# An RWKV-7 and pooling step on one core: 16x16 triangular inverses on VectorE, each pair's first steps begun in the pair ahead, other orders at the front and before the gate

## The chip, the core and the metric

The kernel runs on one core of a Trainium2 chip. Five engines work side by side, each through its own list of instructions: TensorE (PE in the profile; PEld is its weight load), VectorE (DVE), ScalarE (ACT), GpSimd (POOL) and SyncE (SP, which here issues DMAs). They meet at semaphores: an instruction raises one by 1 (a DMA by 16) when it ends, another waits until it has reached a number. The metric is device time of one execution in microseconds (us).

## The reference, cut to what matters

One layer for 256 prompt tokens and 8 short sequences of 8 sample tokens, 320 tokens in all, width 2048, in float32:

```
h = rmsnorm(x);  z = h @ w_in            # r, k, v, g, u, g_pool (1024 columns each), two gates (2048 each)
r, k, v = token shift of z's first 3072 columns
decay = exp(-0.606531*sigmoid(w0 + tanh(xw@w1)@w2));  a = sigmoid(a0 + (xa@a1)@a2)
kk = k*k_k / norm(k*k_k per head);  k = k*(1+(a-1)*k_a)
per head, per token: S = S*diag(decay) - (S kk)(kk*a)^T + v k^T;  o = S r
y_a = (groupnorm(o)*ln_w + ln_b + bonus*v) * silu(g)
y_b = windowed means of u, mapped, * silu(g_pool)
m = sigmoid(gate_a)*(y_a @ wa) + sigmoid(gate_b)*(y_b @ wb)
x = x + rmsnorm(m @ w_out);  x = x + sigmoid(x @ w_ple_gate) * (p @ w_ple)
```

The recurrence is worked in chunks of 64 tokens. Within a chunk the removal terms make a strictly triangular 64x64 matrix A per head, and the chunk needs (I - A)^-1, the matrix Y of the code.

## The kernel before, in words

**Splits.** The big products are taken in three passes: weights and activations are each split into a high and a low part, and hi·hi, hi·lo and lo·hi are added in PSUM. A weight chunk is 8 k-tiles by 128 columns. SP loads it (`wraw`), ACT casts its high part (`wh`, L682), DVE subtracts to get the low part (`wl`, L1017), and PE uses both (L1529 to L1531). There are four slots; ACT and DVE work three chunks ahead (`go(j)`, `ahead`). What PE does for one k-tile of a chunk, three matmuls, is called a unit below.

**Pairs.** The 16 heads are worked as 8 pairs of two heads. Pair r's recurrence runs while PE streams the 6 projection tiles (k, r, v, g, u, g_pool; 96 units) of the pair after it. `mix` exists once per engine. In PE's `mix` the small products stand in the code at fixed places, and `st.advance(AFTER[name])` puts so many units of the stream behind each. `tile_out` (`out(n)`) empties tile n from PSUM on DVE; the stream's next use of that bank waits for it (`acc_free`).

**One pair, in PE's order.** Two products for decay and a (L1632); the key norm (L1637), whose sum DVE takes on with a maximum, ACT with a root and DVE with a reciprocal (L1160); the turned values; the bonus sum (L1647); the products with the initial states (`z`, L1655), which wait for `zr`; the scores (L1661, L1666, L1671), for five groups of 64 tokens, four of the prompt and one of the samples; the turned keys; the inverse; then the chain over the four prompt chunks, outputs, mean (L1756), variance (L1759). The pair's end on DVE is `dO` (L1298), a reciprocal of the deviation (L1306), two steps of the norm, `yf`, and `out(5)` (L1044).

**The inverse.** DVE solves the 8x8 blocks on the diagonal by 23 dependent steps (shuffles within 32 partitions, multiplies, reductions; L1187 to L1245). Then three levels double the block: PE multiplies (`products`, L1688), DVE masks, PE multiplies again (`update`, L1695), DVE adds. The sample group needs none of the levels.

**Beside it.** POOL copies parameters and values, forms `kf`, `sg`, `aS*pi`, `zr`, `kBD`, issues the loads of the next pair and stores states. Before the pairs a front normalises x, transposes and splits h, and streams the first pair's tiles with the two low-rank maps (L1618) beside the later ones. After the pairs come pooling, the merge, the output projection, the last norm and the gate of the per-layer embedding.

Of the kernel before, what the change touches and what calls it, by code (L numbers as in the profile page):

```python
# [28 lines left out]
ds = bass.ds  # L29
# [27 lines left out]
LEVELS = 3  # L57
OCT = 8

# [18 lines left out]
BASE_STEPS = 23  # L78
# [23 lines left out]
def _columns(table, *widths):  # L102
    at = 0
    for name, width in widths:
# [6 lines left out]
                ("batch", NB), ("count", 4 * 16), ("upper", 1), ("lowers", 1), ("unit", 4), ("octs", OCT))  # L111
# [4 lines left out]
def shape_constants():  # L116
# [25 lines left out]
    put(CF, f, "octs", (row // OCT)[:, None] == np.arange(C // OCT)[None])  # L142
# [11 lines left out]
    put(CM, m, "inner", (s // OCT == t // OCT) & (s < t) & seq)  # L154
    a = CM["level"][0]
    for n in range(LEVELS):
        m[:, a + n * TP:a + (n + 1) * TP] = level(OCT * 2 ** n).reshape(P, TP)

# [9 lines left out]
def build(nc, x_prompt, x_sample, state_wkv, state_shift, state_pool, p_prompt, p_sample, norm_pre, norm_post,  # L168
# [3 lines left out]
    with ExitStack() as ctx:  # L172
# [43 lines left out]
        cur_m = r1.take("cur_m", [P, NPAR])  # L216
        lw2 = r1.take("lw2", [RANK, P])
# [66 lines left out]
        O_s, dO, dsq, sd, gsig = cl, pd, pi, kf, rn  # L284
        terms = r1.take("terms", [P, G, 5, 4])
        scratch = Region(used["rn"][0])
        inner = scratch.take("inner", [P, G, OCT])
# [6 lines left out]
        assert scratch.next <= used["rn"][1]  # L294
        parts = at(used["cl"][0], "parts", [P, G, 5, 4])
# [41 lines left out]
        wple0 = r4.take("wple0", [P, 7, 2 * P])  # L337
        wple1 = at(used["cm"][0], "wple1", [P, 5, 2 * P])
# [3 lines left out]
        def embedding_weights(m):  # L342
            if m < 2:
                return wple[:, m, :]
            if m < 9:
                return wple0[:, m - 2, :]
            return wple1[:, m - 9, :] if m < 14 else wple2[:, m - 14, :]
# [20 lines left out]
        for name in """y_out0 y_out1 root_table lo_ready x_in0 x_in1 x_in2 eout sout const_in rows_in rows2_in lora_in map_in filled  # L368
            last_done rows_out cur_p_ready lw2_in s0_in s0d_ready par_done xw_ready xw_used cur_m_ready acc_free vbd_ready
# [4 lines left out]
            vs_ready bt_ps y_ready ybd_ready x_ready base_step kt_ps tail_ps s_ready sd_ready endbd_ready  # L374
# [44 lines left out]
        def _(sp):  # L419
# [18 lines left out]
            row = 0  # L438
            for v in (norm_pre[0].rearrange("(q p) -> q p", p=P), norm_post[0].rearrange("(q p) -> q p", p=P),
                      mu_lora[0].rearrange("a (q p) -> (a q) p", p=P)[0:32, :], pool_scale[0].rearrange("(q p) -> q p", p=P)):  # L440
                n = v.shape[0]
                sp.dma_start(rows[row:row + n, 1, :], v).then_inc(s["rows2_in"], 16)
                row += n
# [55 lines left out]
        def _(pool):  # L499
# [8 lines left out]
            gp_.memset(stat[:, 3:4], 1.0).then_inc(s["filled"], 1)  # L508

            def pair_params(q):  # L510

                gp_.tensor_copy(cur_p[:, :], par[:, :].rearrange("p (n q) -> p n q", q=PAIRS)[:, :, ds(q, 1)]
                                .rearrange("p n q -> p (n q)")).then_inc(s["cur_p_ready"], 1)

# [16 lines left out]
            pair_params(0)  # L531
            pool.wait_ge(s["hT_ps"], 12)
# [22 lines left out]
            def mix(r):  # L555

                gp_.tensor_copy(cur_m[:, :], par[:, :].rearrange("p (n q) -> p n q", q=PAIRS)[:, :, ds(r, 1)]
                                .rearrange("p n q -> p (n q)")).then_inc(s["cur_m_ready"], 1)
                wait_alone("cur_m_ready", r + 1)

                wait_alone("acc_free", r * TILES_STEP + (ACC_STEP + TILES_STEP))
# [10 lines left out]

                wait_alone("sg_ready", r + 1)
                gp_.tensor_tensor(sg[:, :], sg[:, :], gS[:, :], ALU.mult).then_inc(s["sgs_ready"], 1)
# [40 lines left out]
            with pool.Fori(1, PAIRS) as q:  # L615
                r = q - 1
                wait_alone("acc_free", q * TILES_STEP + ACC_STEP)
                pair_params(q)
                mix(r)
# [3 lines left out]
                pair_loads(q)  # L623
                mix_out(r)
# [6 lines left out]
            pool.wait_ge(s["y_done"], PAIRS)  # L631
            pool.dma_start(spt[:, :], state_pool[0].rearrange("b t c -> (b t) c")).then_inc(s["pool_in"], 16)
# [40 lines left out]
        def _(act):  # L673
# [84 lines left out]

            def mix(r, q):
# [7 lines left out]
                go(0)  # L767
                act.wait_ge(s["cur_m_ready"], r + 1)
                A.activation(sq[:, :], kS[:, :], ACT.Square, scale=cur_m[:, K_K:K_K + 1]).then_inc(s["ksq_ready"], 1)
                act.wait_ge(s["lora2_ps"], r + 1)  # L770
                A.activation(pm[:, :], B[0][:, 0:T], ACT.Sigmoid, bias=cur_m[:, W0:W0 + 1]).then_inc(s["decay_in"], 1)
                A.activation(aS[:, :], B[1][:, 0:T], ACT.Sigmoid, bias=cur_m[:, A0:A0 + 1]).then_inc(s["a_ready"], 1)
                A.activation(sg[:, :], gS[:, :], ACT.Sigmoid).then_inc(s["sg_ready"], 1)
                act.wait_ge(s["kk_max"], r + 1)
                A.activation(rn[:, :], rn[:, :], ACT.Sqrt).then_inc(s["kk_norm"], 1)
                act.wait_ge(s["cum_ready"], r + 1)
                A.activation(pi[:, :], cl[:, :], ACT.Exp, scale=DECAY).then_inc(s["exp_ready"], 1)
# [29 lines left out]

                act.wait_ge(s["bt_ps"], r + 1)
                A.copy(BtBD[:, :, :, :].rearrange("p g h c -> p (g h c)"), B45[:, 0:2 * TP])

                act.wait_ge(s["kt_ps"], r + 1)
                A.copy(KtBD[:, :, :, :].rearrange("p g h c -> p (g h c)"), B23[:, 0:2 * TP])
                for n in range(LEVELS):
                    go(4 + n)
                out(2)
                go(4 + LEVELS)
# [193 lines left out]
        def _(dve):  # L1010
# [12 lines left out]
            def tile_out(q, n):  # L1023
# [13 lines left out]
                else:  # L1037
# [4 lines left out]
                    else:  # L1042
                        dve.wait_ge(s["gsig_ready"], q)
                        V.tensor_tensor(t[:, where], bank, gsig[:, :], ALU.mult).then_inc(s["acc_free"], 1)  # L1044
# [46 lines left out]
            for c in range(4):  # L1091
# [3 lines left out]
                if c == 0:  # L1095
                    split_lo(0, 0)
            split_lo(0, 1)
            split_lo(0, 2)

# [15 lines left out]
            split_lo(0, 3)  # L1115
# [23 lines left out]

            def mix(r, q):  # L1140
                def go(j):
                    ahead(q * CH_STEP + BASE_STEP, j)
# [4 lines left out]
                go(0)  # L1147
                dve.wait_ge(s["s0_in"], r * 128 + 128)
                for h in range(2):
                    V.transpose(S0T[half(h), :, half(h)], S0n[half(h), :, :]).then_inc(s["s0t_ready"], 1)  # L1150

                dve.wait_ge(s["kk_ps"], r + 1)
                V.tensor_scalar(rn[:, :], B[2][:, 0:T], 1e-24, None, ALU.max).then_inc(s["kk_max"], 1)

                dve.wait_ge(s["decay_in"], r + 1)
# [102 lines left out]
                for n in range(LEVELS):  # L1258
# [5 lines left out]
                    if n == 2:  # L1264
                        out(2)
# [695 lines left out]
```

## Time and profile before

| | |
|---|---|
| median of 3 runs (lowest to highest) | 1218.7 us (1217.64 to 1219.46) |
| profiled execution | 1217.77 us, of which the span of its instructions is 1216.2 us |
| PE busy | 1188.5 us, 98% of the span |
| DVE, ACT, POOL busy | 730.3 us (60%), 544.1 us (45%), 198.5 us (16%) |
| mean granted TensorE clock | 0.997 of full speed |
| share of the end chain on PE | 93% |

The span runs from the first to the last instruction. "Idle before" and the bracket behind a row say how long the engine had stood still before that instruction and what ended the stand. PE's matmuls are pipelined and their ends are modelled, so a PE that is shown busy can still hold short waits; those are found from the distance between the starts of two products and the units between them.

### The profile page before, as it was taken

Reading aid. Unit: us, or ns where it says so; the run is one execution under the profiler, and the core shown is the slowest. Engines: PE = TensorE matmul, PEld = TensorE weight load, DVE = VectorE, ACT = ScalarE, POOL = GpSimd, SP = SyncE. Lnnn points to the kernel's source line nnn. Section 1 sums busy time; section 2 is a strip of 40 time slices with the busy share of each in tenths; the row PEclk is TensorE's granted clock in tenths of the full one; section 3 lists DMA queues with packets and bytes.
Section 4 is the critical chain, followed back from the end, with each engine's and each line's share of the span. In section 5 each row is a group of like instructions: output and inputs, shape, how many; then the busy total and the mean of one; then the engine's idle time right before and its main releaser. Section 6 shows DMA issues by size and latency. Waiting matters only on the chain.

```text
span 1216.2 us, 21935 instructions
## 1 busy us (share of the span) xinstructions
PE 1188.5 (98%) x8060; PEld 1142.6 (94%) x8060; DVE 730.3 (60%) x1246; ACT 544.1 (45%) x875; POOL 198.5 (16%) x305
## 2 busy tenths in 40 slices
PE   4999999999999999999999999999999999999998
PEld 3789999999999999999999999999999999979998
DVE  6858584857668585867758744444444354475442
ACT  5244463737364563736353333333333343345342
POOL 3233141504123150503122000000000400000000
PEclk8999999999999999999999999999999999999999
DMA  9714333332433434332445465554545964424551
GB/s 231 191 53 117 97 98 105 90 103 80 131 96 98 113 84 117 91 104 79 122 116 171 122 173 145 148 152 141 155 138 156 253 189 138 138 71 132 160 160 49
DMA packets 279770, 155.37 MB, mean 128 GB/s; under 512 B 7717, under 2 KB 275661, under 8 KB 279076
## 3 DMA queue, kind: packets, MB, share of 16 engines
q1 hardware_dynamic: 272528, 139.65, 41.0%
q0 software_dynamic: 7056, 15.17, 5.0%
q8 instruction: 25, 0.41, 0.1%
q14 instruction: 13, 0.11, 0.0%
q10 hardware_dynamic: 148, 0.04, 0.0%
HBM read 149.45 MB, written 5.61 MB: 127 GB/s over the span
## 4 chain that ended last, share of the span: by engine, by line
PE 93%; DVE 3%; DMA 2%; ACT 1%; issue 0%; POOL 0%; SPq 0%; ACTq 0%; DVEq 0%; POOLq 0%
PE acc L1529 19%; PE acc L1530 19%; PE acc L1531 18%; PE wide L1531 5%; PE wide L1530 5%; PE wide L1529 5%; PE wide L1548 2%; PE wide L1695 2%; PE wide L1688 2%; PE wide L1618 1%; PE wide L1903 1%; PE wide L1655 1%; DMA pt<-in_p_sample 1%; PE wide L1661 1%; PE wide L1743 1%; PE wide L1666 1%
## 5 line engine op out<-in xcount | busy, mean ns | idle before, releaser
L1017 DVE TENSOR_TENSOR wl<-wraw,wh 128x1024 fp32r<-128x1024 f32 x256 | 313.7, 1230 | 219.7 <-ACT wh L682 212.1
L682 ACT CAST wh<-wraw 128x1024 fp32r<-128x1024 f32 x256 | 266.8, 1047 | 246.5 <-PE acc L1531 153.6
L1529 PE MATMUL acc<-hh,wh 128*128 128x320 f32 (+1 forms) x1084 | 362.1, 334 | 2.7 <-DVE wl L1017 2.7
L1530 PE MATMUL acc<-hl,wh 128*128 128x320 f32 (+1 forms) x1084 | 336.6, 311 | 0.0
L1531 PE MATMUL acc<-hh,wl 128*128 128x320 f32 (+1 forms) x1084 | 336.2, 310 | 0.0
L1529 PEld LDWEIGHTS acc<-hh,wh 128*128 128x128 f32 x1084 | 204.7, 189 | 6.7 <-issue 3.2
L1530 PEld LDWEIGHTS acc<-hl,wh 128*128 128x128 f32 x1084 | 204.5, 189 | 3.4
L1531 PEld LDWEIGHTS acc<-hh,wl 128*128 128x128 f32 x1084 | 203.9, 188 | 0.0
L1529 PE MATMUL acc<-x1h,wh 128*128 128x320 f32 x256 | 82.5, 322 | 0.4 <-DVE x1l L1486 0.4
L1529 PE MATMUL acc<-mh,wh 128*128 128x320 f32 x256 | 80.6, 315 | 0.0
L1531 PE MATMUL acc<-x1h,wl 128*128 128x320 f32 x256 | 79.1, 309 | 0.0
L1531 PE MATMUL acc<-mh,wl 128*128 128x320 f32 x256 | 79.1, 309 | 0.0
L1530 PE MATMUL acc<-ml,wh 128*128 128x320 f32 x256 | 79.1, 309 | 0.0
L1530 PE MATMUL acc<-x1l,wh 128*128 128x320 f32 x256 | 79.1, 309 | 0.0
L1531 PE MATMUL wide<-hh,wl 128*128 128x320 f32 x192 | 59.5, 310 | 0.0
L1530 PE MATMUL wide<-hl,wh 128*128 128x320 f32 x192 | 59.3, 309 | 0.0
L1529 PE MATMUL wide<-hh,wh 128*128 128x320 f32 x192 | 59.2, 308 | 0.0
L660 POOL DMA_DIRECT2D xt<-in_x_prompt x1 | 0.6, 557 | 301.6 <-PE wide L1531 301.6
L1529 PEld LDWEIGHTS acc<-x1h,wh 128*128 128x128 f32 x256 | 48.1, 188 | 1.4 <-DVE x1l L1486 0.7
L1529 PEld LDWEIGHTS acc<-mh,wh 128*128 128x128 f32 x256 | 48.0, 188 | 0.9
L1530 PEld LDWEIGHTS acc<-x1l,wh 128*128 128x128 f32 x256 | 48.1, 188 | 0.7
L1530 PEld LDWEIGHTS acc<-ml,wh 128*128 128x128 f32 x256 | 48.1, 188 | 0.0
(361 smaller groups left out, 2178.9 us busy)
## 6 DMA issues: line engine op xcount, KB each, us to landing
wraw<-in_w_in SPq DMA_DIRECT2D x160, 512.0 KB, 3.8
wraw<-in_w_branch SPq DMA_DIRECT2D x32, 512.0 KB, 4.0
wraw<-in_w_out SPq DMA_DIRECT2D x32, 512.0 KB, 4.0
wraw<-in_w_ple_gate SPq DMA_DIRECT2D x32, 512.0 KB, 4.1
xt<-in_x_prompt SPq DMA_DIRECT2D x2, 1024.0 KB, 6.9
S0n<-in_state_wkv POOLq DMA_DIRECT2D x64, 32.0 KB, 4.3
out<-so POOLq DMA_DIRECT2D x16, 128.0 KB, 2.8
xt<-in_x_prompt POOLq DMA_DIRECT2D x2, 1024.0 KB, 7.6
```

The lines of the kernel that those rows point to most:

```text
L682: A.copy(wh[:, slot, :], wraw[:, slot, :]).then_inc(s["hi_ready"], 1)
L1017: V.tensor_tensor(wl[:, slot, :], wraw[:, slot, :], wh[:, slot, :].bitcast(F32), ALU.subtract).then_inc(s["lo_ready"], 1)
L1529: M.matmul(out[:, 0:width], wh[:, slot, wcol], hi, start=first, stop=False)
L1530: M.matmul(out[:, 0:width], wh[:, slot, wcol], lo, start=False, stop=False)
L1531: return M.matmul(out[:, 0:width], wl[:, slot, wcol], hi, start=False, stop=last)
L1548: return M.transpose(out, in_, ident[0:rows, 0:rows])
L1618: M.matmul(B[n % 2][0:RANK, 0:T], (lw1, la1)[n % 2][:, k, :], xw[:, n % 4, :], start=k == 0, stop=k == KT - 1).then_inc(s["xw_used"], 1)
L1655: last = M.matmul(B45[:, P * b:P * b + 2 * TB + C], S0T[:, b, :], zr[:, b, :], start=True, stop=True)
L1661: last = M.matmul(B01[:, P * g:P * (g + 1)].rearrange("p (a c) -> p a c", a=2), flat(bBD, g), ar[:, :, tok(g)], start=True, stop=True)
L1666: last = M.matmul(B23[:, P * g:P * (g + 1)].rearrange("p (a c) -> p a c", a=2), flat(kBD, g), ar[:, :, tok(g)], start=True, stop=True)
L1688: last = M.matmul(B[0][:, tok(g)], flat(ABD, g), Y[:, g, :], start=True, stop=True)
L1695: last = M.matmul(B[1][:, tok(g)], flat(XBD, g), Tm[:, g, :], start=True, stop=True)
```

## The change

**Inverse.** `LEVELS` goes from 3 to 2. DVE solves 16x16 blocks: the 8x8 solution is followed by one more doubling on DVE, with 24 more steps (`BASE_STEPS` 23 to 47), among them 16 shuffles of 40 columns. `ABD` and the third score group are formed for the four prompt groups only. `ARK` and `AKBD` move out of that chain into the two levels; the weight splits go(4) and out(1) move into it.

**Pair.** The key squares, decay, a and gate sigmoids of the next pair (ACT: `key_squares`, `decays`, `gates`), and the turned states, norm maximum, running sum and its difference (DVE: `states_turned`, `decays`) stand inside the pair ahead. POOL takes the next pair's first parameters once `out(2)` of this one is done, copies the values after `out(4)`, and has a small third copy, `cur_n`, for the norm's weights. The units behind PE's places change with it. The key transposes move behind the first `products`.

**Front and ramp.** The four parameter rows go from SP's queue to POOL's. DVE splits weight chunks 1 and 3 earlier. Before the gate, two of the embedding products stand ahead of the sum for the last norm.

```
-LEVELS = 3
+LEVELS = 2
+HEX = 16
...
-            AFTER = dict(maps=13, key_norm=6, values=4, bonus=9, scores=8, keys=2, product=3,
-                         update=2, chain_rhs=2, chain_u=2, chain_state=1, mean=4, chain_end=3, inner=6)
+            AFTER = dict(maps=2, key_norm=8, values=10, bonus=9, scores=30, product=3,
+                         update=2, chain_rhs=2, chain_u=2, chain_state=1, mean=3, chain_end=3)
...
-                for g in range(G):
+                for g in range(GP):
                     last = M.matmul(B[4][:, tok(g)], flat(aBD, g), bU[:, tok(g)], start=True, stop=True)
...
+                stepped(25)
+                dve.sem_inc(s["waits"], 1)
+                for k in range(OCT):
+                    V.stream_shuffle(rows8[:, :, k, :], octo[:, :, :], hex_row(OCT + k)).then_inc(s["base_step"], 1)
+                V.tensor_scalar(sixteen[:, :, 0:OCT], octo[:, :, :], cfs("upper8"), None, ALU.mult).then_inc(s["base_step"], 1)
+                V.tensor_scalar(parts8[:, :, OCT, :], octo[:, :, :], cfs("lower8"), None, ALU.mult).then_inc(s["base_step"], 1)
+                stepped(33)
+                V.tensor_tensor(parts8[:, :, 0:OCT, :], cross16[:, :, :].unsqueeze(3).to_broadcast([P, G, OCT, OCT]),
+                                rows8[:, :, :, :], ALU.mult).then_inc(s["base_step"], 1)
+                stepped(36)
+                V.tensor_reduce(half16[:, :, :], parts8[:, :, 0:OCT, :].rearrange("p g k j -> p g j k"), mybir.AxisListType.X,
+                                ALU.add).then_inc(s["base_step"], 1)
+                go(4)
+                stepped(37)
+                dve.sem_inc(s["waits"], 1)
+                for k in range(OCT):
+                    V.stream_shuffle(rows8[:, :, k, :], half16[:, :, :], hex_row(k)).then_inc(s["base_step"], 1)
...
+                if more:
+                    states_turned(q)
 
                 dve.wait_ge(s["mean_ps"], r + 1)
                 V.tensor_tensor(dO[:, :], O_s[:, :], B[5][:, 0:T], ALU.subtract).then_inc(s["dev_ready"], 1)
...
                 V.reciprocal(sd[:, :], sd[:, :]).then_inc(s["dve_step"], 1)
+                if more:
+                    decays(q)
...
+                more = not isinstance(q, int)
+                if more:
+                    key_squares(q)
                 act.wait_ge(s["var_ps"], r + 1)
                 A.activation(sd[:, :], B[2][:, 0:T], ACT.Sqrt, bias=cfs("eps")[:, 1:2]).then_inc(s["sd_done"], 1)
+                if more:
+                    decays(q)
                 act.wait_ge(s["chunk_used"], q * CH_STEP + (BASE_STEP + 12))
-                A.activation(gsig[:, :], acc[1][:, 0:T], ACT.Sigmoid).then_inc(s["gsig_ready"], 1)
-
+                A.activation(gsig, acc[1][:, 0:T], ACT.Sigmoid).then_inc(s["gsig_ready"], 1)
+                if more:
+                    gates(q * TILES_STEP + 3)
...
             pool.wait_ge(s["y_done"], PAIRS)
+            pool.wait_ge(s["acc_free"], ACC_ALL)
             pool.dma_start(spt[:, :], state_pool[0].rearrange("b t c -> (b t) c")).then_inc(s["pool_in"], 16)
...
             for i in range(FRONT):
+                if i == 2:
+                    pe.wait_ge(s["sacc_ready"], KT)
+                    M.matmul(B[5][:, 0:T], meand, sacc[:, :], start=True, stop=True).then_inc(s["ssq_ps"], 1)
                 embedding(i)
```

On VectorE, at the end of a pair and the start of the next one (`pd` is `dO`, `gp` the pool gate of `out(5)`, `wl` a weight split), the list reads before:

```order
L1306 RECIPROCAL kf<-kf 128x320
L1308 SCALAR_TENSOR_TENSOR pd<-pd,cur_m,kf 128x320
...
L1313 TENSOR_TENSOR yf<-pd,sg 128x320
...
L1044 TENSOR_TENSOR gp<-acc,rn 128x320
...
L1017 TENSOR_TENSOR wl<-wraw,wh 128x1024
L1150 STREAM_TRANSPOSE S0T<-S0n 64x8x64 x2
L1153 TENSOR_SCALAR rn<-wide 128x320
L1156 SCALAR_TENSOR_TENSOR cl<-cf,pm 128x320
L1158 TENSOR_TENSOR pm<-cl,pm 128x320
L1160 RECIPROCAL rn<-rn 128x320
L1163 SCALAR_TENSOR_TENSOR sq<-rS,cur_m,kf 128x320
L1166 SCALAR_TENSOR_TENSOR kkn<-kS,cur_m,rn 128x320
```

and now:

```order
L1389 RECIPROCAL kkn<-kkn 128x320
...
L1192 TENSOR_SCALAR rn<-wide 128x320
L1194 SCALAR_TENSOR_TENSOR cl<-cf,pm 128x320
L1196 TENSOR_TENSOR pm<-cl,pm 128x320
L1394 SCALAR_TENSOR_TENSOR pd<-pd,cur_n,kkn 128x320
...
L1399 TENSOR_TENSOR yf<-pd,sg 128x320
...
L1087 TENSOR_TENSOR gp<-acc,Tm 128x320
...
L1208 RECIPROCAL rn<-rn 128x320
L1211 SCALAR_TENSOR_TENSOR sq<-rS,cur_m,kf 128x320
L1060 TENSOR_TENSOR wl<-wraw,wh 128x1024
L1215 SCALAR_TENSOR_TENSOR kkn<-kS,cur_m,rn 128x320
```

The next pair's maximum, running sum and difference now stand between the first pair's reciprocal and its norm; the turned states have gone further ahead, and the weight split has gone behind `sq`.

On VectorE in the front (`hl` is the low part of h, `dh` the token difference), before:

```order
L1093 TENSOR_TENSOR hl<-hT,hh 128x1312
L1017 TENSOR_TENSOR wl<-wraw,wh 128x1024
L1093 TENSOR_TENSOR hl<-hT,hh 128x1312 x3
L1017 TENSOR_TENSOR wl<-wraw,wh 128x1024 x2
...
L1113 TENSOR_TENSOR dh<-hT 128x16x8
L1017 TENSOR_TENSOR wl<-wraw,wh 128x1024 x2
L1033 SCALAR_TENSOR_TENSOR kS<-acc,cur_p,zsh 128x320
```

and now:

```order
L1136 TENSOR_TENSOR hl<-hT,hh 128x1312
L1060 TENSOR_TENSOR wl<-wraw,wh 128x1024
L1136 TENSOR_TENSOR hl<-hT,hh 128x1312
L1060 TENSOR_TENSOR wl<-wraw,wh 128x1024
L1136 TENSOR_TENSOR hl<-hT,hh 128x1312 x2
L1060 TENSOR_TENSOR wl<-wraw,wh 128x1024 x2
...
L1156 TENSOR_TENSOR dh<-hT 128x16x8
L1060 TENSOR_TENSOR wl<-wraw,wh 128x1024
L1076 SCALAR_TENSOR_TENSOR kS<-acc,cur_p,zsh 128x320
```

The same nine steps lead to `kS`; the second split has moved two places up and the fourth ahead of the differences.

On TensorE, at the last norm (`m` is the output projection's input, `wple` are the embedding's weights, `acc` the gate's first tile), before:

```order
L1530 MATMUL acc<-ml,wh 128x320
L1531 MATMUL acc<-mh,wl 128x320
L1881 MATMUL wide<-sacc,cf 128x320
L1903 MATMUL wide<-pT,wple 128x320 x4
L1903 MATMUL wide<-pT,wple_167 128x320 x12
L1529 MATMUL acc<-x1h,wh 128x320
```

On TensorE at the same place now:

```order
L1618 MATMUL acc<-ml,wh 128x320
L1619 MATMUL acc<-mh,wl 128x320
L1987 MATMUL wide<-pT,wple 128x320 x4
L2000 MATMUL wide<-sacc,cf 128x320
L1987 MATMUL wide<-pT,wple_174 128x320 x12
L1617 MATMUL acc<-x1h,wh 128x320
```

Two embeddings (four products) have gone ahead of the product that waits for the sum.

## Rows read from the trace of the kernel before

**Rows 1.** Busy time by stretch, one pair: us, engines, PE clock, DMA share, GB/s

```profile
284.20:353.20 69.00, 68.99 (x488) 66.03 (x487) 48.45 (x101) 37.41 (x67) 19.01 (x28) 1.00 0.37 101
```

**Rows 2.** Timeline of PE in that pair: start us, us, operation, [idle before]

```profile
278.27 0.70 PE L1756 MATMUL wide<-cl,cf 128*128 128x320 f32 x2
...
280.58 0.70 PE L1759 MATMUL wide<-pi,cf 128*128 128x320 f32 x2
...
284.21 0.70 PE L1632 MATMUL wide<-t,lw 96*128 96x320 f32 x2
...
301.71 1.98 PE L1655 MATMUL wide<-zr,S0T 128*128 128x80 f32 x16
...
305.81 1.23 PE L1671 MATMUL wide<-bU,aBD 128*128 128x64 f32 x10
...
315.03 1.00 PE L1688 MATMUL wide<-Y,ABD 128*128 128x64 f32 x8
...
323.23 1.00 PE L1688 MATMUL wide<-Y,ABD 128*128 128x64 f32 x8
```

**Rows 3.** Timeline of DVE in that pair

```profile
283.26 2.15 DVE L1306 RECIPROCAL kf<-kf 128x320 f32<-128x320 f32 x1 [0.62 <-ACT kf L850]
...
287.15 0.48 DVE L1044 TENSOR_TENSOR gp<-acc,rn 128x320 f32 x1
...
291.89 0.49 DVE L1153 TENSOR_SCALAR rn<-wide 128x320 f32<-128x320 f32 x1 [1.77 <-PE wide L1637]
...
294.34 2.14 DVE L1160 RECIPROCAL rn<-rn 128x320 f32<-128x320 f32 x1
...
296.78 1.15 DVE L1166 SCALAR_TENSOR_TENSOR kkn<-kS,cur_m,rn 128x320 f32<-128x320 f32 x1
...
304.89 0.49 DVE L1187 TENSOR_TENSOR Tm<-wide,cm 128x320 f32<-128x320 f32 x1
...
313.19 0.49 DVE L1245 TENSOR_TENSOR Y<-octo,cf 128x320 f32<-128x320 f32 x1
```

**Rows 4.** Timeline of DVE in the first pair

```profile
89.79 0.55 DVE L1166 SCALAR_TENSOR_TENSOR kkn<-kS,cur_m,rn 128x320 f32<-128x320 f32 x1
```

**Rows 5.** Timeline of POOL in the pair of rows 2

```profile
296.66 0.92 POOL L577 TENSOR_TENSOR aS<-aS,pi 128x320 f32<-128x320 f32 x1 [1.51 <-ACT pm L780]
...
299.02 1.98 POOL L584 TENSOR_TENSOR kBD<-kf,pi 64x320 f32<-64x320 f32 x2 [0.18 <-POOL zr L580]
```

**Rows 6.** Groups of DVE's instructions: xcount, busy us, mean ns, idle us before

```profile
L1194 DVE TENSOR_REDUCE inner<-Tm 128x40 f32<-128x320 f32 x8 | 5.9, 732 | 0.3
...
L1237 DVE STREAM_SHUFFLE rows4b<-half_way 128x20 f32<-128x20 f32 x32 | 3.7, 175 | 0.1
```

**Rows 7.** Page, costliest groups: the weight split

```profile
L1017 DVE TENSOR_TENSOR wl<-wraw,wh 128x1024 fp32r<-128x1024 f32 x256 | 313.7, 1230 | 219.7 <-ACT wh L682 212.1 <-POOL S0T L551 5.6
```

**Rows 8.** Timeline of PE at the end of the last pair

```profile
632.07 1.03 PE L1548 MATMUL wide<-cf,uS 128*79 128x128 f32 x8
```

**Rows 9.** Timeline of DVE at the end of the last pair

```profile
631.43 0.48 DVE L1044 TENSOR_TENSOR gp<-acc,rn 128x320 f32<-128x320 f32 x1
```

**Rows 10.** Waits of PE: us in total, times, longest

```profile
PE acc L1529 <- DVE wl L1017: 2.7, 2, 1.4
```

**Rows 11.** Timeline of PE in the front

```profile
40.86 0.39 PE L1529 MATMUL acc<-hh,wh 128*128 128x328 f32 x1 [1.32 <-DVE wl L1017]
```

**Rows 12.** Timeline of DVE in the front

```profile
41.76 0.54 DVE L1033 SCALAR_TENSOR_TENSOR kS<-acc,cur_p,zsh 128x320 f32<-128x320 f32 x1
```

**Rows 13.** Timeline of ACT in the front

```profile
16.14 1.92 ACT L714 ACTIVATE junk<-xt 64x2048 f32<-64x2048 f32 x1 [1.23 <-DMA xt<-in_state_shift]
```

**Rows 14.** Timeline of PE before the gate

```profile
1074.72 0.81 PE L1881 MATMUL wide<-sacc,cf 128*128 128x320 f32 x2 [1.59 <-DVE sacc L1455]
...
1083.74 0.55 PE L1529 MATMUL acc<-x1h,wh 128*128 128x320 f32 x1
```

**Rows 15.** Timeline of DVE before the gate

```profile
1080.95 0.83 DVE L1486 TENSOR_TENSOR x1l<-xT,x1h 128x640 fp32r<-128x640 f32 x1 [0.22 <-ACT x1h L959]
```

More of the change, by code:

```diff
@@ L216, in build @@
         cur_m = r1.take("cur_m", [P, NPAR])
+        cur_n = r1.take("cur_n", [P, 2])
         lw2 = r1.take("lw2", [RANK, P])
@@ L294, in build @@
         assert scratch.next <= used["rn"][1]
+        scratch = Region(used["pm"][0])
+        parts8 = scratch.take("parts8", [P, G, OCT + 1, OCT])
+        oct_in = scratch.take("oct_in", [P, G, OCT])
+        cross16 = scratch.take("cross16", [P, G, OCT])
+        half16 = scratch.take("half16", [P, G, OCT])
+        sixteen = scratch.take("sixteen", [P, G, HEX])
+        assert scratch.next <= used["aS"][1]
+        rows8 = at(used["kkn"][0], "rows8", [P, G, OCT, OCT])
         parts = at(used["cl"][0], "parts", [P, G, 5, 4])
@@ L508, in _ @@
             gp_.memset(stat[:, 3:4], 1.0).then_inc(s["filled"], 1)
+            row = 0
+            for v in (norm_pre[0].rearrange("(q p) -> q p", p=P), norm_post[0].rearrange("(q p) -> q p", p=P),
+                      mu_lora[0].rearrange("a (q p) -> (a q) p", p=P)[0:32, :], pool_scale[0].rearrange("(q p) -> q p", p=P)):
+                n = v.shape[0]
+                pool.dma_start(rows[row:row + n, 1, :], v).then_inc(s["rows2_in"], 16)
+                row += n
             def pair_params(q):
@@ L806, in mix @@
                 out(1)
+                go(4)
+                go(5)
+                out(2)
                 act.wait_ge(s["bt_ps"], r + 1)
[L809 to L816, printed above, removed]
+                A.copy(BtBD[:, :, :, :].rearrange("p g h c -> p (g h c)"), B[4][:, :]).then_inc(s["keys_ready"], 1)
+                A.copy(KtBD[:, :, :, :].rearrange("p g h c -> p (g h c)"), B[5][:, :]).then_inc(s["keys_ready"], 1)
+                go(6)
+                go(7)
                 act.wait_ge(s["y_ready"], r * (LEVELS + 1) + LEVELS + 1)
@@ L1673, in mix @@
                 st.advance(AFTER["scores"])
-                pe.wait_ge(s["ark_ready"], r + 1)
-                for g in range(GP):
-                    last = transpose(B45[:, P * g:P * (g + 1)], flat(bBD, g))
-                last.then_inc(s["bt_ps"], 1)
-                st.advance(AFTER["keys"])
-                for g in range(GP):
-                    last = transpose(B23[:, P * g:P * (g + 1)], flat(kBD, g))
-                last.then_inc(s["kt_ps"], 1)
                 def products(n):
@@ L1696, in update, with turned_keys @@
                     last.then_inc(s["m_ps"], 1)
-                st.advance(AFTER["inner"])
+                def turned_keys():
+                    for t, bank in ((bBD, B[4]), (kBD, B[5])):
+                        for g in range(GP):
+                            last = transpose(bank[:, P * g:P * (g + 1)], flat(t, g))
+                    last.then_inc(s["bt_ps"], 1)
+                pe.wait_ge(s["ark_ready"], r + 1)
                 for n in range(LEVELS):
```

211 lines of the change are left out of this document (127 added, 84 removed).

## The prediction

> **What bounds the kernel now.** First the page's busy times: PE is busy for 98% of the span and 93% of the end chain lies on it. Then the busy time by stretch: in one pair, 69.0 us long, PE is busy for 68.99 at clock 1.00, DVE for 48.45 and ACT for 37.41 [rows 1]. So a pair lasts as long as PE's list does, as long as nothing is late for it. Then PE's timeline, for what a unit and a small product cost: from mean to variance, 278.27 to 280.58, lie one such product and 4 units, from variance to maps, 284.21, the same product and 7 [rows 2]. Three units more cost 3.63 − 2.31 = 1.32, so a unit costs 0.44 us and the product 0.55. Last the timelines of DVE and POOL, for the chains that have to end before a place of PE [rows 3 to 9], and the front and the ramp, where PE does wait [rows 10 to 15].
>
> The change takes work off PE in each pair and gives DVE some more. It gains what PE drops, unless DVE becomes late. All sums are made against the profiled execution, 1217.77 us, which is 0.93 below the median of the runs; 0.93 is added at the end.
>
> **PE's work, gain 17.0.** Two of the three levels take 323.23 − 315.03 = 8.20 us [rows 2], one 4.10. Of that 5 units (3 behind `products`, 2 behind `update`) are stream and only move: 2.20. The level itself goes, 1.90. The third score group falls from ten products (1.23 us) to eight, and eight of that shape take 1.00 [rows 2]: 0.23. Together 2.13 a pair, 17.0 over 8 pairs. Small hidden waits inside the levels that stay may go as well; I leave them out.
>
> **The head of a pair, cost 3.2.** PE's slot from mean to `z` was 301.71 − 278.27 = 23.44 us with 43 units (4, 7, 13, 6, 4 and 9 behind mean, variance, maps, key norm, values and bonus). Now it holds 34 (3, 2, 2, 8, 10, 9): 9 × 0.44 = 3.96 less, 19.5. In this slot DVE has to bring `zr`, by a chain that now has no idle in it. Its pieces, from [rows 3]: the reciprocal of the deviation starts 283.26 − 278.27 = 5.0 behind the mean; I take 5.2, since ACT now squares the next keys ahead of the root. From there to the end of `gp` 4.37 (283.26 to 287.63). Maximum, running sum and difference, which now stand among these steps, 2.45 (291.89 to 294.34). Reciprocal and `sq` 2.44 (294.34 to 296.78). The weight split go(0), now behind `sq`, 1.23 [rows 7]. `kkn` to `z` 4.93 (296.78 to 301.71). Sum 20.6: PE would stand 1.1 at `z`.
>
> The last piece is what the two ends hang on. `kkn` took 1.15 in this pair and 0.55 in the first [rows 3, 4]; in this pair POOL worked on `aS`, `zr` and `kBD` from 296.66 to 301.00 beside it [rows 5]. Four such steps, each 0.6 shorter, make 18.2 and no stall. POOL's block waits for the exponentials, which come off the running sum; that one is now ready before the norm's steps, the split and `kkn`, so the block should start some 14 us behind the mean and end at 18, while `kkn` starts at 15.7: a little over half of the piece would still lie beside POOL. This takes off about 0.8: chain 19.8, stall 0.3, and 0.1 for ZaBD, which comes off the same steps ahead of the third score group. I take 0.4 a pair, 3.2 in all. Ends: 0 and 2.9 (three two-input steps of the norm each 0.6 longer, because POOL's block would reach them: 22.4 against 19.5).
>
> The Trainium skill ("SBUF — State Buffer", Who interferes with whom) says that a VectorE instruction with two SBUF inputs contends with a GpSimd instruction that reads SBUF, since the shared port pair is locked for a whole instruction, and that one with at most one SBUF input doesn't. By that rule, the 1.15 against 0.55 agrees with it, and a head packed with two-input steps beside POOL speaks against this change; it is the mechanism of the last rival below.
>
> **The inverse, cost 0.** Mask to Y took 313.68 − 304.89 = 8.79 [rows 3]. Out of it go `AKBD` and `ARK`, at least one 320-wide step of 0.49 each: −1.0. In come 16 shuffles of 40 columns, by the nearest row 0.175 each (2.8), though the small ones start every 0.1 us (1.5); two products of 320 at 0.49; two reductions at 0.73 [rows 6]; four small steps, about 0.9; a split of 1.23 and out(1), 0.54. Waits between dependent steps: 0.4. That makes 14.3 to 15.6, say 15, and 17 if each shuffle and wait is paid in full. PE's slot from `z` to the first products was 315.03 − 301.71 = 13.32. It gets 14 units more (30 behind the scores in place of 8, 2 and 6 behind the scores, the first keys and the second): +6.2; the eight key transposes leave it (eight of another tile take 1.03 [rows 8]), and 0.23 of the score group: 18.3. Mask starts 3.2 behind `z`, so Y is there at 17.5 to 18.8, and 20.2 at worst. I take 0; ends 0 and 1.9 a pair.
>
> **Mean to variance, cost 0.** With 3 units PE's slot is 0.55 + 1.32 = 1.87. The deviation and its square took under 1.9 with ACT free; they just fit. At most 0.5 a pair if they don't.
>
> **The end of the pairs, cost 2.2.** In the last pair PE reaches the transposes for pooling 6 units or 2.65 us sooner after its mean than before, because fewer units stand behind the variance. The last `out(5)` ended at 631.91 [rows 9], 0.16 ahead of the transposes at 632.07 [rows 8]: no spare time. DVE drops only the next pair's steps, which the last pair never had, and at most 0.3 elsewhere. So PE waits some 2.2 there. The load of the pool's states now also waits for that tile. Ends 1.0 and 3.0.
>
> **The front, gain 1.5.** PE waits 2.7 us for two weight splits, 1.4 at most in one [rows 10]; the second ends at 40.86 [rows 11]. Both splits come earlier now. But `kS` empties the bank that the third tile needs, it ended at 42.30 [rows 12], and the same steps lead to it. The third tile came 8 units (3.6 us) behind 40.86, at 44.4; 2.7 sooner it would be 41.7, so PE waits there for 0.6. Gain 0 to 2.1; I take 1.5, since the maps' inputs are late as well.
>
> **x, gain 0.6.** ACT waited 1.23 for the last rows of x [rows 13], behind the four parameter rows on SP's queue, which now go by POOL's. Bounds 0 and 1.2; half.
>
> **The ramp, gain 1.3.** PE waited 1.59 for the sum, then did it and eight embeddings, 1075.37 to 1083.74, 1.05 each [rows 14]. Two of them now stand inside the wait: 2.1 against 1.59, so the sum comes 0.5 later and all of it ends 1.59 sooner. The gate's input `x1l` was ready at 1081.78 [rows 15], now at about 1082.3, and the gate starts at 1082.2 to 1082.4. Ends 0 and 1.6.
>
> **Sum.** 1217.77 − 17.0 + 3.2 + 2.2 − 1.5 − 0.6 − 1.3 = 1202.8; with 0.93, 1203.7 us.
>
> **Rivals.**
>
> A. The head chain binds fully: POOL's block lies on all of the piece from `kkn` to `z` and a step more, 1.1 to 2.0 us a pair. For it: nothing idles in that chain any more. Against it: the block starts sooner. 1203.7 + (1.3 − 0.4) × 8 = 1211, from 1209 to 1216.
>
> B. The inverse is late by 1 to 2 us, because 24 dependent small steps are dearer than my nearest rows. For it: the sum leaves PE's slot 0.5 us at most. Against it: short shuffles start every 0.1 us. 1203.7 + 1.2 × 8 = 1213, from 1211 to 1220.
>
> C. Nothing is late: `kkn` and its like run at 0.55, the hidden waits in the levels go, and the end of the pairs costs 1. 1203.7 − 3.2 − 1.2 − 3 = 1196.
>
> D. Slower. DVE becomes the bound of the head: POOL's and DVE's two-input steps meet along all of the head, from the norm's steps to `zr`, and the stall at `z` is 2.9 us or more, while mean to variance no longer fits. 1203.7 + (2.9 − 0.4 + 0.2) × 8 = 1225. It decides from a stall of (1218.7 − 1203.7) / 8 + 0.4 = 2.3 a pair. For it: 1.15 against 0.55. Against it: POOL's 19 us a pair [rows 1] leave most of the pair alone.
>
> **How the numbers follow.** Forecast 56%, A 17%, B 11%, C 8%, D 8%. The forecast's own range is 1198 to 1209, by the ends of the end of the pairs, front, ramp and ±0.4 a pair. The range for 8 in 10 is 1195 to 1216: it takes in C's value and A, and leaves out D, B's upper part and a tail of C. A measurement of this kernel tells about 0.2%, 2.4 us, from no change: faster means below 1216.3. Forecast, C, nearly all of A and two thirds of B lie there: 0.88. Within 0.2%: the top of A and B and the foot of D, 0.04. Slower 0.08.
>
> **What would show it.** Right: a pair of about 67.3 us with two levels; PE's distance from mean to `z` at 19.5 to 20.2; Y ready at most a few tenths behind PE's arrival at the first products; a wait of some 2 us at the transposes behind the last pair; a new wait for `kS` in the front in place of those for the splits; no wait at the sum before the gate. Wrong: a listed wait of PE for `zr` or Y of over 1 us in every pair (A, B or D; POOL beside `kkn` tells A and D, a Y later than 19 us behind `z` tells B), or a pair under 66.9 (C).

## The result, and the profile after

The changed kernel takes 1201.4 us (median of 4 runs, 1200.65 to 1203.95), the one before, run beside it, 1219.08: ratio 0.9864, interval 0.9853 to 0.9876. That is faster, 2.3 us below the forecast of 1203.7 and within its range. The sum was nearly right for reasons that were only partly right. The profiled execution, 1203.95 us with a span of 1202.4, is the longest of the four; it holds one late transfer, which is later in some executions than in others (below).

PE's waits in the profile after (us in total, times, longest):

```profile
...
PE wide L1636 <- POOL vBD L580: 2.7, 1, 2.7
PE wide L1744 <- issue: 2.3, 6, 0.4
PE wide L1636 <- DVE gp L1087: 1.9, 1, 1.9
PE wide L1636 <- DMA pt<-in_p_sample: 1.6, 1, 1.6
...
PE acc L1617 <- DVE kS L1076: 0.8, 1, 0.8
...
```

Of the rows shown, the second, the third and the last were forecast: `z`, the tail behind the last pair, `kS` in the front. The first was not. The fourth is the transfer: PE's transposes of x wait for a group of six loads, and the last of them, for `pt` (the input p of the embedding), landed 12.3 us behind its issue here, 10.8 in the trace of before.

Busy time of one steady pair after, from mean to mean, to set beside [rows 1]:

```profile
269.60:336.33 66.73, 66.36 (x469) 64.06 (x468) 51.24 (x137) 34.31 (x64) 21.82 (x29) 1.00 0.38 104
```

A pair has become 69.00 − 66.73 = 2.27 us shorter, where 1.73 were forecast, and PE now stands 0.37 us in it. Its places on PE's timeline, to set beside [rows 2]:

```profile
270.04 0.70 PE L1845 MATMUL wide<-cl,cf 128*128 128x320 f32 x2
271.89 0.74 PE L1848 MATMUL wide<-pi,cf 128*128 128x320 f32 x2
...
289.68 1.98 PE L1744 MATMUL wide<-zr,S0T 128*128 128x80 f32 x16 [0.37 <-issue]
...
308.13 1.00 PE L1767 MATMUL wide<-Y,ABD 128*128 128x64 f32 x8
...
312.99 1.00 PE L1767 MATMUL wide<-Y,ABD 128*128 128x64 f32 x8
...
316.97 0.38 PE L1636 MATMUL wide<-cf,tail 128*128 128x128 f32 x2
```

And the second and third level on PE in the kernel before; the prediction took the third from the first two:

```profile
319.01 1.00 PE L1688 MATMUL wide<-Y,ABD 128*128 128x64 f32 x8
...
321.36 1.10 PE L1695 MATMUL wide<-Tm,vBD 128*128 128x64 f32 x8
...
323.23 1.00 PE L1688 MATMUL wide<-Y,ABD 128*128 128x64 f32 x8
...
327.46 0.38 PE L1548 MATMUL wide<-cf,tail 128*128 128x128 f32 x2
```

DVE in the same pair after, to set beside [rows 3]:

```profile
283.59 1.90 DVE L1060 TENSOR_TENSOR wl<-wraw,wh 128x1024 fp32r<-128x1024 f32 x1
285.42 1.34 DVE L1215 SCALAR_TENSOR_TENSOR kkn<-kS,cur_m,rn 128x320 f32<-128x320 f32 x1
286.90 0.93 DVE L1219 SCALAR_TENSOR_TENSOR ar<-kkn,pm 128x320 f32<-128x320 f32 x1
287.76 1.16 DVE L1221 TENSOR_TENSOR bU<-kkn,aS 128x320 f32<-128x320 f32 x1
288.84 0.48 DVE L1222 TENSOR_TENSOR ar<-rS,pd 128x320 f32<-128x320 f32 x1
...
292.86 0.49 DVE L1236 TENSOR_TENSOR Tm<-wide,cm 128x320 f32<-128x320 f32 x1
...
306.57 0.49 DVE L1319 TENSOR_TENSOR Y<-sixteen,cf 128x320 f32<-128x320 f32 x1
```

POOL beside it, to set beside [rows 5]:

```profile
283.37 1.05 POOL L598 TENSOR_TENSOR aS<-aS,pi 128x320 f32<-128x320 f32 x1 [0.51 <-ACT pm L814]
...
286.59 1.98 POOL L605 TENSOR_TENSOR kBD<-kf,pi 64x320 f32<-64x320 f32 x2 [0.18 <-POOL zr L601]
```

POOL's block has come ahead, as forecast; it now ends at 288.57. The last step, `ar` from `rS`, is free of it and takes 0.48. But the split, which was priced at 1.23, takes 1.90.

Where the time went, by stretches between the same places of PE in both profiled executions (the first mean is the start of its first product, the last mean that of its second):

| stretch | before | after | difference |
|---|---|---|---|
| start to the first pair's maps | 77.33 | 73.73 | −3.6 |
| to the first mean | 62.9 | 62.8 | −0.1 |
| first to last mean (7 pairs) | 482.7 | 470.5 | −12.2 |
| to the transposes behind the last pair [rows 8] | 9.2 | 8.7 | −0.5 |
| to the transposes of the pool's states | 4.7 | 6.0 | +1.4 |
| to the end | 579.5 | 580.7 | +1.2 |

The seven pairs hold one that isn't steady, the last. PE's timeline there, and at the end of the pairs, after:

```profile
549.17 1.33 PE L1636 MATMUL wide<-cf,vBD 128*128 128x128 f32 x5 [2.66 <-POOL vBD L580]
...
615.66 1.10 PE L1636 MATMUL wide<-cf,uS 128*79 128x128 f32 x8 [1.92 <-DVE gp L1087]
...
617.27 0.47 PE L1617 MATMUL acc<-hh,wh 128*128 128x320 f32 x1
617.53 0.47 PE L1618 MATMUL acc<-hl,wh 128*128 128x320 f32 x1
...
620.33 0.31 PE L1617 MATMUL acc<-hh,wh 128*128 128x320 f32 x1
620.48 0.31 PE L1618 MATMUL acc<-hl,wh 128*128 128x320 f32 x1
```

The granted clock in the stretches right behind these stands, and behind the one for `pt` (the last number but two of each row), after:

```profile
549.17:555.44 6.27, 6.27 (x36) 6.27 (x36) 4.95 (x5) 3.51 (x8) 5.37 (x6) 0.78 0.10 30
...
615.66:621.70 6.04, 6.04 (x32) 5.89 (x32) 2.79 (x2) 4.30 (x6) 5.46 (x12) 0.72 0.68 157
...
951.00:954.00 3.00, 3.00 (x13) 2.99 (x13) 0.00 (x0) 0.45 (x2) 0.00 (x0) 0.54 1.08 295
```

Behind each of the three, PE ran for some microseconds at half speed (1.2 GHz): a matmul starts every 0.26 us in place of 0.15. From the value transposes to the bonus a steady pair takes 284.55 − 279.48 = 5.07, here 6.27: 1.2 lost beside the 2.66. At the tail 6.04 against 4.67 before: 1.4 beside the 1.92.

The same stand is not followed by such a dip every time. Of the eight traces that have the stand at the value transposes (the changed kernel's and seven of the experiments', 2.64 to 2.66 us each), seven have the dip and one, that of the splits in the old order, has not:

```profile
551.38:556.40 5.02, 5.02 (x35) 5.02 (x36) 3.75 (x4) 3.52 (x8) 4.30 (x5) 1.00 0.01 3
```

Of the ten with the stand of 1.9 at the tail, four have it. In the six others PE stands 0.9 to 1.3 us for the load of the pool's states instead, one of them in best_a:

```profile
616.57 1.04 PE L1635 MATMUL wide<-cf,spt 120*128 120x120 f32 x8 [1.31 <-DMA spt<-in_state_pool]
```

So the tail takes nearly the same time either way: from the transposes behind the last pair to those of the pool's states 5.99 to 6.04 with the dip and 5.52 to 5.94 without.

### The profile page after: what moved, and what is told of

The parts are those of the page before. It is cut to its first block, busy times and chain, and to the rows that moved or that the text cites. A ratio compares the mean times of both kernels' runs of the same rounds, so it can differ in the third digit from the quotient of the medians.

```text
span 1202.4 us, 22093 instructions
## 1 busy us (share of the span) xinstructions
PE 1171.7 (97%) x7916; PEld 1131.2 (94%) x7916; DVE 755.1 (63%) x1534; ACT 523.2 (44%) x862; POOL 213.7 (18%) x317
## 4 chain that ended last, share of the span: by engine, by line
PE 92%; DVE 3%; DMA 2%; issue 1%; ACT 1%; POOL 0%; DVEq 0%; ACTq 0%; POOLq 0%
PE acc L1617 19%; PE acc L1618 19%; PE acc L1619 19%; PE wide L1619 5%; PE wide L1618 5%; PE wide L1617 5%; PE wide L1636 3%; PE wide L1706 1%; PE wide L1987 1%; PE wide L1744 1%; PE wide L1774 1%; PE wide L1767 1%; DMA pt<-in_p_sample 1%; PE wide L1750 1%; PE wide L1832 1%
## 5 line engine op out<-in xcount | busy, mean ns | idle before, releaser
L1060 DVE TENSOR_TENSOR wl<-wraw,wh 128x1024 fp32r<-128x1024 f32 x256 | 318.4, 1249 | 210.6 <-ACT wh L708 209.0
L1619 PEld LDWEIGHTS acc<-mh,wl 128*128 128x128 f32 x256 | 48.7, 190 | 0.0
```

The costliest lines, as they stand in the source:

```text
L1060: V.tensor_tensor(wl[:, slot, :], wraw[:, slot, :], wh[:, slot, :].bitcast(F32), ALU.subtract).then_inc(s["lo_ready"], 1)
L1619: return M.matmul(out[:, 0:width], wl[:, slot, wcol], hi, start=False, stop=last)
```

## The experiments

Two things are read from each: the ratio to the kernel before, whose median was 1217.8 to 1218.1 us in these runs, and distances in the trace, since the changed kernel's own runs spread by 3 us. Where two ratios lie within each other's interval, the trace decides and not the median. "Changed" is the changed kernel.

**The values of the last pair.** In the loop POOL waits for five of the six tiles, up to `out(4)`, before it copies the next pair's values; the pair written out behind the loop still had a wait for all six.

```
-            pool.wait_ge(s["acc_free"], PAIRS * TILES_STEP + ACC_STEP)
             mix(PAIRS - 1)
```

> The changed kernel, but POOL no longer waits for the last tile of the pair ahead before it copies the last pair's values (the eighth, written-out pair has that wait; the loop's seven don't). Theory 1: that wait alone makes PE stand 2.7 us at the value transposes of the last pair; without it the stand is gone and the median falls from 1201.4 by 2.7 to about 1198.7. Rival: the stand is given back later in the same pair, since the scores or z of that pair then wait for DVE's chain, which isn't sooner; then 1200.5 to 1201.5, and a wait for z of 1 us or more in the last pair.

1199.6 us, ratio 0.9857 (0.9842 to 0.9872). The stand at the value transposes is gone, and the clock's dip behind it. Part of it comes back at `z` of that pair. ACT and PE in that pair:

```profile
548.82 1.28 ACT L810 ACT_TABLE_LOAD   x1 [1.22 <-DVE gp L1086]
```

```profile
557.51 1.98 PE L1743 MATMUL wide<-zr,S0T 128*128 128x80 f32 x16 [1.50 <-issue]
```

First to last mean is 2.4 shorter: 2.7 and 1.2 less, 1.5 more. Both theories had a part; the time fits neither's number well enough to choose by it, the trace does. The rest shows how little room the head has: in this pair ACT's table load for the exponentials waits for `gp`, which was ready 11.8 behind the mean. In a steady pair `gp` is ready at 11.2, and the table load starts at 10.7, ahead of it. So the first exponential starts 13.15 behind the mean in place of 11.95, and the stand at `z` is 1.50 in place of 0.37.

**The tail behind the last pair.**

```
             def last_rows():
-                pe.wait_ge(s["acc_free"], ACC_ALL)
...
+            pe.wait_ge(s["acc_free"], ACC_ALL)
             for g in range(1, 4):
```

> The changed kernel, but the transposes behind the last pair don't wait for out(5), which they don't read; that wait stands ahead of the second gate instead. Theory 1: the 1.9 us stand at these transposes goes, and with it the dip of the granted clock right behind it (about 1.4 us): 1198.1. Rival: the pool's states, loaded only when the last pair's values are out, land 5.4 us behind their issue, at 621.65, so PE stands for them instead, some 3.5 us, and nothing is gained: 1200.5 to 1202, with the dip behind the later stand.

1203.1 us, 0.9872 (0.9857 to 0.9887): nothing gained, and the rival's stand is there.

```profile
622.41 0.90 PE L1636 MATMUL wide<-cf,spt 120*128 120x120 f32 x5 [3.15 <-DMA spt<-in_state_pool]
```

The wait for `out(5)` was not what set the end of the pairs; the load of the pool's states, which starts when the last values are out, is as late: it waits for `out(5)` too.

**One unit moved.**

```
-bonus=9, scores=30
+bonus=10, scores=29
```

> The changed kernel with one unit moved from behind the scores to behind the bonus (10 and 29 in place of 9 and 30). Theory 1: PE's stand of 0.38 us at z in each pair is a true wait for DVE; a unit of 0.44 us covers it, Y has 1.0 us to spare, so 0.38 x 7 or 8, 2.7 to 3.0 us, go: 1198.5. Rival: the stand is no wait for DVE but a shift that comes back at the scores (ZaBD, bv) or at the first products; then within 0.5 of 1201.4 with a new stand there.

1198.55 us, 0.9849 (0.9836 to 0.9863). No wait at `z` is listed any more, first to last mean is 467.6 in place of 470.5, and nothing new appears. Theory 1, by the trace; the ratio alone doesn't tell it from the changed kernel.

**Five score groups.**

```
-                for g in range(GP):
+                for g in range(G):
                     last = M.matmul(B[4][:, tok(g)], flat(aBD, g), bU[:, tok(g)], start=True, stop=True)
```

> The changed kernel with the third score group formed for five groups again (its fifth result isn't read). Theory 1: two more products of 0.12 us on PE in each pair, 0.23 x 8 = 1.9 us: 1203.3. Rival: PE stands a little later anyway, so they are hidden: 1201.4.

1204.9 us, 0.9893 (0.9878 to 0.9908). First to last mean is 472.3 against 470.5, 0.26 a pair: theory 1. The median rose by more than that; its trace also has a wait of 1.1 for the pool's states, the one that all six traces without the dip at the tail have, and 0.9 for `pt`. What made the median rise by 3.5 is not shown beyond the 1.9 of the products.

**A level less, in the kernel before.** Two levels, 5 units more ahead of the first, and the splits go(6), go(7) and out(2) behind the levels.

```
-LEVELS = 3
+LEVELS = 2
...
-inner=6)
+inner=11)
```

> The kernel before with one doubling level left out (two in place of three; the inverse stays block-wise incomplete), its 5 units put ahead of the first level; nothing else of the change. Theory 1: the level alone is worth what its instructions take on PE, 4.23 - 5 x 0.442 = 2.0 us a pair by the trace of before (the prediction said 1.90), 16 us in all: 1202. Rival: a level hides DVE's work that then has to be waited for, so a pair gives back a third or more: 1207 to 1212.

1209.8 us, 0.9930 (0.9916 to 0.9943): 8 us, half of what the level's instructions take; a steady pair takes 68.0 in place of 69.0. One wait of PE is new:

```profile
PE wide L1723 <- DVE RHS L1274: 4.6, 8, 0.7
```

So the rival. DVE's splits of the third level have to go somewhere; here they stood right ahead of `RHS`, so the wait is in part of this edit's making. Here a level's worth on PE was had in full only where DVE's work in it found a place: the change put go(4) and out(1) inside its longer inverse.

**The parameter rows back on SP.** The four issues stand ahead of the second part of x again.

> The changed kernel with the four parameter rows back on SP's queue ahead of the second and third part of x. Theory 1: these four issues alone hold back x, and with it all the front: PE's first product with h comes 2.0 us later (25.2 in place of 23.1) and the time rises to 1203.4. Rival (the prediction's number): x gains 0.6, the rest of the front's 3.6 us is the earlier weight splits: 1202.0, first product with h at 23.7.

1203.2 us, 0.9873 (0.9858 to 0.9888). PE's first product with h, in this kernel:

```profile
25.74 0.64 PE L1687 MATMUL acc<-hh,wh 128*128 128x328 f32 x1 [2.32 <-DVE hl L1136]
```

In the changed kernel it starts at 23.14, in the one before at 25.19; the maps come at 76.3 against 73.7. That is theory 1's direction and a little more than its number. But the place moves by itself: among the eleven traces with the rows on POOL it lies at 23.1 to 24.0 in ten and at 25.13 in best_b's, where nothing in the front was edited; with the rows on SP it lies at 25.19, 25.39 and 25.74. So the rows are worth some 2 us in most executions, and the size is not known to better than about 1.

**The front's splits in the old order.**

```
-                if c < 2:
-                    split_lo(0, c)
-            split_lo(0, 2)
-            split_lo(0, 3)
+                if c == 0:
+                    split_lo(0, 0)
+            split_lo(0, 1)
+            split_lo(0, 2)
...
+            split_lo(0, 3)
```

> The changed kernel with the weight splits of the front in the old order. Theory 1 (the prediction): the two waits for splits, 2.7 us, come back and the waits for kS (0.8) and the maps' input (0.5) go: 1.5 slower, 1202.9. Rival: the waits for kS and the maps stay too, since x and not the splits sets the front: 1204.

1202.4 us, 0.9873 (0.9857 to 0.9888). Waits of 1.00 and 1.35 for splits are back, those for `kS` and the maps' input (0.76 and 0.45) are gone: 1.1 from these alone. The distance from PE's first product with h to the maps says more, since it hardly moves between executions: 52.14 here and in the kernel before, 50.56 to 50.59 in all eleven traces with the new order. The difference is 1.55. Theory 1, and its number. The median, 1.0 above the changed kernel's, is within the spread.

**The sum first, before the gate.**

```
-                if i == 2:
+                if i == 0:
                     pe.wait_ge(s["sacc_ready"], KT)
```

> The changed kernel with all embeddings behind the sum for the last norm again. Theory 1: PE's stand of 1.6 us for the sum comes back and all behind it moves: 1203.0. Rival: the gate's input, not the embeddings, sets the start of the gate, so the stand is covered: 1201.4 to 1201.9.

1203.0 us, 0.9875 (0.9860 to 0.9890), and the wait is back:

```profile
PE wide L2000 <- DVE sacc L1543: 1.7, 1, 1.7
```

Theory 1.

**The next pair's maximum and sum late.**

```
                 V.reciprocal(sd[:, :], sd[:, :]).then_inc(s["dve_step"], 1)
-                if more:
-                    decays(q)
...
                 out(5)
+                if more:
+                    decays(q)
```

> The changed kernel with the next pair's maximum, running sum and difference on DVE behind out(5), as before the change, not between the deviation's reciprocal and the norm. The sum of DVE's work in the head is the same. Theory 1: ACT's root and exponentials and with them POOL's block start some 2 us later, so POOL lies beside all steps from kkn to zr, each 1.15 and none 0.5, and the reciprocal of the norm waits for ACT's root (about 0.8): the stand at z grows from 0.38 to between 1.5 and 2.5, the time to 1209 to 1216. Rival: only DVE's sum counts: the stand stays near 0.4, 1201 to 1202.

1203.45 us, 0.9884 (0.9869 to 0.9900). The durations came as theory 1 has them, the time did not. DVE and PE in that kernel:

```profile
285.13 1.21 DVE L1060 TENSOR_TENSOR wl<-wraw,wh 128x1024 fp32r<-128x1024 f32 x1
286.26 1.15 DVE L1215 SCALAR_TENSOR_TENSOR kkn<-kS,cur_m,rn 128x320 f32<-128x320 f32 x1
...
289.68 1.16 DVE L1222 TENSOR_TENSOR ar<-rS,pd 128x320 f32<-128x320 f32 x1
```

```profile
281.16 0.74 PE L1636 MATMUL wide<-cf,vBD 128*128 128x128 f32 x5 [0.54 <-DVE rn L1192]
...
291.20 1.98 PE L1744 MATMUL wide<-zr,S0T 128*128 128x80 f32 x16 [0.21 <-issue]
```

POOL lies beside all four steps, 0.6 on each, 2.5 in all; but the split is free of it, 1.21. In the changed kernel the split lost 0.7, `kkn` 0.8, the first `ar` 0.4 and `bU` 0.6: also 2.5. In both traces POOL's block costs DVE the same, on whichever two-input steps it falls, and the split is one of them. What the edit does cost is a new stand of 0.54 at the value transposes, whose bank the later maximum still holds. Five of the six steady pairs take 67.2 to 67.3 in place of 66.75, 2.6 us in all. First to last mean grows by 0.9 alone, since the last pair is 1.7 shorter: POOL's stand there is 2.0, and no dip follows in this execution. So the median is 2 us higher, and not 8 or more. My theory fell on its size, and the ACT root that it added was hidden.

**POOL's block shortened.**

```
-gp_.tensor_tensor(kBD[half(h), :, h, :], grp(kf)[half(h)], grp(pi)[half(h)],
+gp_.tensor_tensor(kBD[half(h), 0:1, h, :], grp(kf)[half(h), 0:1, :], grp(pi)[half(h), 0:1, :],
```

> The changed kernel with POOL's product kBD formed for one of five groups of tokens (the rest is left out), nothing else: POOL's last step of the block, 1.98 us, falls to about 0.6. Theory 1 (VectorE's two-input steps are slow because POOL reads beside them): bU falls from 1.16 to about 0.5, ar from 0.93 to about 0.55, the chain to z by about 1 us, the stand of 0.38 goes: 1198.5. Rival: they are slow for their own operands (bU reads what ACT and POOL just wrote); then bU stays at 1.16 and the stand at 0.38: 1201.4.

1198.5 us, 0.9847 (0.9834 to 0.9861), no wait at `z`, and DVE reads:

```profile
284.92 1.34 DVE L1215 SCALAR_TENSOR_TENSOR kkn<-kS,cur_m,rn 128x320 f32<-128x320 f32 x1
286.41 0.49 DVE L1219 SCALAR_TENSOR_TENSOR ar<-kkn,pm 128x320 f32<-128x320 f32 x1
286.82 0.61 DVE L1221 TENSOR_TENSOR bU<-kkn,aS 128x320 f32<-128x320 f32 x1
```

Same operands and other durations: theory 1. That POOL's work beside them, and not what they read, makes these steps slow is shown here.

**Better than both.** best_a is the changed kernel with the edits of the last pair's values and of the moved unit.

> The changed kernel with two of the edits: no wait of POOL for the last tile ahead of the last pair's values, and the one unit from the scores to the bonus. The gains stand in different pairs, so they add, apart from the last pair's z, where the moved unit covers 0.44 of the 1.5 us that the first edit left: by the traces 2.4 + 2.7 + 0.4 = 5.5 less, 1196. Rival: the moved unit only shifts the last pair's new stand: 1197 to 1198.

1195.8 us (1195.17 to 1196.41), 0.9815 (0.9801 to 0.9828): theory 1. First to last mean 464.9, and at the last pair's `z` PE stands 0.95 in place of 1.50. best_b adds the tail:

```
             early_gate(0, 1)
+            pe.wait_ge(s["acc_free"], ACC_ALL)
+            early_gate(1, 0)
             pe.wait_ge(s["pool_in"], 16)
```

> As best_a, and the transposes behind the last pair don't wait for out(5), while the transposes of the pool's states stand behind one more gate chunk (3.5 us), when those have landed. Theory 1: the 1.9 us stand and the clock's dip behind it (1.4) go and no new stand comes: 3.3 below best_a, about 1193. Rival: VectorE takes its splits in order behind the copy of the pool's states, which now comes one chunk later for PE, so PE waits for splits: no gain over best_a.

1195.95 us, 0.9811 (0.9795 to 0.9828), one run at 1191.85. The stand at the tail and the one for the states are gone from its trace, and behind the last mean PE starts the transposes that wait for `pt` 2.6 us sooner than in best_a's, with a wait of 1.4 for `pt` in place of 0.7. Behind that wait the clock dipped, which cost 1.5, and the front of this execution was 1.4 later, where nothing was edited. So a gain is there up to `pt`, and what it is worth in time stays open.

## Why the prediction came out, point by point

- **What bounds it**: right. PE stays at 97 to 98% and a pair follows PE's list. But a pair of 66.73 lies under 66.9, which the prediction had named as a sign against itself and for its rival C. Of C's three conditions one came true, the hidden waits in the levels; `kkn` did not run at 0.55, and the end of the pairs cost more than 1.
- **PE's work, 2.13 a pair**: too small, by 0.5 a pair or 4 in all. Without the stand a pair lost 2.27 + 0.37 = 2.64. The step that failed is the level, taken as half of the first two, and "small hidden waits ... I leave them out". The third took 327.46 − 323.23 = 4.23, without its units 2.0. The two that stay, without the key transposes that now lie in them (0.87), fell from 8.20 to 316.97 − 308.13 − 0.87 = 7.97. The hidden waits show level by level: before, the first took 319.01 − 315.03 = 3.98 and the two behind it 4.22 and 4.23, in each of which the second product came late for DVE's mask; now both take 3.98 to 3.99. The head lost 0.2 more than its units and its stand account for. The score group was right (0.26 measured, 0.23 said).
- **The head, 0.4 a pair**: right in size, 0.37, and the chain from mean to `z` was 289.68 − 270.04 = 19.64 against 19.8. That is luck in part. From the deviation's reciprocal to the end of `gp`, with maximum, running sum and difference, 6.1 passed for 6.8; the split, priced as if nothing lay beside it, took 1.83 of the chain for 1.23; `kkn` to `z` took 4.26 for 4.13, so POOL's earlier block did take off what was said, but the split paid it back. The Trainium skill ("SBUF — State Buffer", Who interferes with whom) says that any VectorE instruction with two SBUF inputs contends with a GpSimd instruction that reads SBUF, and the split has two; the traces agree, 1.90 with POOL beside it and 1.21 without. There the Trainium skill frees an instruction with at most one SBUF input only outside the two-port modes, a condition that the prediction's sentence leaves out; nothing in its sum uses that.
- **The inverse, 0**: right. Mask to Y took 307.06 − 292.86 = 14.2, and PE came 1.07 behind Y. The prediction's rows add up to 14.8 to 16.1, where it wrote 14.3 to 15.6; with the right sum its upper end would have cost PE 1.0 a pair. What was measured is less than either. Mean to variance, 1.85 against 1.87: right.
- **The end of the pairs, 2.2**: the stand of 1.9 was there. What came behind it, 1.4, was not in the sum: here the clock's dip, in traces without the dip a stand of 0.9 to 1.3 for the pool's states. The step that was too cheap is the load of the states: the prediction says that it now waits for `out(5)`, and gives it no price. Without the stand at `out(5)` PE waits 3.15 for that load.
- **What the prediction had no term for**: POOL in the last pair, 2.66 and 1.2 of clock, 3.9 (2.7 in an execution without the dip). The loop's wait was changed and the one behind the loop was not; I followed DVE and PE through the last pair and not POOL.
- **The front**: x was mis-sized, about 2 for 0.6 (2.05 between the two profiled executions). I bounded it by ACT's wait for the last rows of x [rows 13]; the wait that shrank is ACT's for the second part of x, 3.9 us in the trace of before and 0.9 after; in best_b's trace it is 3.75, so the rows alone don't decide it. The splits were said to give 1.5 and gave 1.55: right.
- **The ramp, 1.3**: 1.8 to 1.9. From the transposes that wait for `pt` to the end the kernel before takes 249.4, the changed order without a dip there 247.6, and the sum put first 249.5.

In the profiled execution: −2.64 × 8 + 0.37 × 6 + 3.9 + 3.3 − 3.6 − 1.8 = −17.1. The late `pt` cost 1.56, and 1.5 by the clock behind it: from the transposes behind it to the product for the sum 113.25 passed, in traces without that dip 111.7. That makes −14.0, and −13.8 is measured. Other runs are 2.0 to 3.3 us shorter than that execution. That they lack the late transfer is argued and not shown: of the other eleven traces of the changed kernel with one edit or more, seven wait 0 to 0.7 for `pt` and four 0.9 to 1.6. The forecast of −15.0 is the sum of gains that were 6.1 too small (26.5 for 20.4) and costs that were 4.0 too small (9.4 for 5.4). That these nearly cancel is luck.

## What to carry to other kernels

When a wait inside a loop is loosened, read every engine's list through the copy that is written out behind the loop: there the old wait was worth more than the stands at `z` of all pairs together. Price a two-input step on VectorE by whether GpSimd works beside it, and count the overlap of the whole block, since moving it only changes which step pays. And a stand of PE of 1.2 to 2.7 us can cost 1.2 to 1.5 more in clock, or nothing: the same stand at the same place did both. With such dips and late transfers in some executions, a median of four or five runs doesn't decide 1 or 2 us; the distance between two places of PE does.

## What the runs showed of the hardware

After stands of 2.66, 1.92 and 1.56 us PE's granted clock fell to means of 0.54 to 0.78 in the rows behind them, at 1.2 to 1.5 us each, and once after a stand of 1.19 (`pt` in the trace of the parameter rows on SP). After the stand of 1.59 for the sum in the kernel before [rows 14] it was 1.00 throughout the next 4 us, and after one of 1.59 for `pt`, in the trace of the late maximum, too. The stand of 1.9 at the tail was followed by half speed (1.2 GHz) in four traces and by 1.00 in six. So neither the length of the stand nor its place decides it here; what does, no run shows. Shuffles of 40 columns started every 0.11 us, though each is shown 0.19 long.
